# Mixture-of-experts on chip: experts ranked by load, the four emptiest in 64 slots with high and low parts side by side, interleaved chunk by chunk with 128-slot experts

## The reference

```python
def swiglu(h, wg, wu, wd):
    return (jax.nn.silu(h @ wg) * (h @ wu)) @ wd

def moe_swiglu(h, w_router, wg, wu, wd):
    xt = h.reshape(-1, D)                       # 256 x 1024
    logits = (xt @ w_router).astype(jnp.float32)
    top_v, top_i = lax.top_k(logits, TOP_K)     # 2 of 8 experts
    gates = jax.nn.softmax(top_v, axis=-1)
    gate = jnp.sum(jax.nn.one_hot(top_i, N_EXPERTS, ...) * gates[..., None], axis=1)
    for e in range(N_EXPERTS):                  # wg, wu: 1024 x 3584; wd: 3584 x 1024
        y = y + gate[:, e:e + 1] * swiglu(xt, wg[e], wu[e], wd[e])
```

## Time and profile before

| What | Value |
|---|---|
| Median of 3 runs | 1669.54 us (1669.48 to 1670.12) |
| Span of the profiled execution, first to last instruction | 1666.4 us |
| PE busy | 1623.5 us, 97% |
| PEld, DVE, ACT busy | 1347.1, 1317.3, 1082.2 us |
| Mean granted PE clock | 0.988 |
| Read from HBM | 460.18 MB, 277 GB/s over the span |

### The profile page before, as it was taken

The page is one execution under the profiler, slowest core; times in us unless marked ns, Lnnn a source line. Parts: engine busy times, 40 slices in busy tenths (PEclk is TensorE's granted clock), DMA queues, the critical chain, the costliest instruction groups (busy, mean ns, idle before and its releaser), DMA issues.

```text
span 1666.4 us, 20534 instructions
## 1 busy us (share of the span) xinstructions
PE 1623.5 (97%) x7691; PEld 1347.1 (81%) x7691; DVE 1317.3 (79%) x1520; ACT 1082.2 (65%) x1315; POOL 122.1 (7%) x244
## 2 busy tenths in 40 slices
PE   6999999999999996999999999999999999999996
PEld 5788888888888885888888888888888888888884
DVE  4776676575554567898998998998998998998997
ACT  4664574644443562777777777776776776777774
POOL 3433432010000101000000000000000000000000
PEclk9999999999999997999999999999999999999998
DMA  9547445446465633799999999999999999999993
GB/s 347 184 130 216 142 135 177 132 141 202 131 215 189 208 102 102 267 373 381 359 370 337 354 367 371 362 367 333 353 369 373 354 375 338 355 369 355 374 363 131
DMA packets 152928, 462.58 MB, mean 278 GB/s; under 512 B 7870, under 2 KB 12236, under 8 KB 152700
## 3 DMA queue, kind: packets, MB, share of 16 engines
q1 hardware_dynamic: 150384, 454.32, 75.5%
q0 software_dynamic: 1824, 5.11, 1.2%
q10 hardware_dynamic: 620, 1.83, 0.3%
HBM read 460.18 MB, written 1.05 MB: 277 GB/s over the span
## 4 chain that ended last, share of the span: by engine, by line
PE 93%; DVE 3%; DMA 2%; DVEq 1%; issue 1%; ACT 1%; SPq 0%; ACTq 0%
PE ps L2324 19%; PE ps L2322 19%; PE ps L2323 18%; PE ps L1840 8%; PE ps L1842 8%; PE ps L1841 8%; DMA raw_sb<-w_in 2%; PE ps L2349 1%; PE ps L2258 1%; PE ps L1886 1%; PE ps L1888 1%; PE ps L1887 1%; PE ps L1921 0%; DVE wlo_sb L1132 0%; PE ps L1865 0%
## 5 line engine op out<-in xcount | busy, mean ns | idle before, releaser
L1140 DVE TENSOR_TENSOR wlo_sb<-raw_sb,whi_sb 128x1024 fp32r<-128x1024 f32 x672 | 789.0, 1220 | 96.6 <-ACT whi_sb L818 95.5
L818 ACT ACTIVATE whi_sb<-raw_sb 128x1024 fp32r<-128x1024 f32 x672 | 674.9, 1053 | 243.3 <-PE ps L2324 243.3
L2322 PE MATMUL ps<-whi_sb,xlo_sb 128*128 128x512 f32 x896 | 351.2, 392 | 0.9 <-ACT xhi_sb L1076 0.9
L2324 PE MATMUL ps<-whi_sb,xhi_sb 128*128 128x512 f32 x896 | 349.1, 390 | 0.0
L2323 PE MATMUL ps<-wlo_sb,xhi_sb 128*128 128x512 f32 x896 | 348.9, 389 | 0.0
L1132 DVE TENSOR_TENSOR wlo_sb<-raw_sb,whi_sb 128x1024 fp32r<-128x1024 f32 (+2 forms) x198 | 230.1, 1204 | 143.0 <-ACT whi_sb L810 142.0
L810 ACT ACTIVATE whi_sb<-raw_sb 128x1024 fp32r<-128x1024 f32 (+2 forms) x198 | 192.3, 1022 | 160.4 <-PE ps L1842 131.2
L1840 PE MATMUL ps<-whi_sb,xlo_sb 128*128 128x512 f32 (+2 forms) x544 | 213.1, 392 | 4.0 <-DVE xlo_sb L1179 4.0
L1842 PE MATMUL ps<-whi_sb,xhi_sb 128*128 128x512 f32 (+2 forms) x544 | 209.0, 384 | 0.0
L1841 PE MATMUL ps<-wlo_sb,xhi_sb 128*128 128x512 f32 (+2 forms) x544 | 208.7, 384 | 0.0
L2322 PEld LDWEIGHTS ps<-whi_sb,xlo_sb 128*128 128x128 f32 x896 | 168.3, 188 | 35.3 <-issue 1.1
(11 more groups left out here) (351 smaller groups left out, 1514.4 us busy)
## 6 DMA issues: line engine op xcount, KB each, us to landing
raw_sb<-moe_wg SPq DMA_DIRECT2D x115, 1024.0 KB, 5.8
raw_sb<-moe_wu SPq DMA_DIRECT2D x112, 1024.0 KB, 6.0
raw_sb<-moe_wd SPq DMA_DIRECT2D x112, 1024.0 KB, 6.3
raw_sb<-w_in SPq DMA_DIRECT2D x40, 1024.0 KB, 5.2
raw_sb<-w_out SPq DMA_DIRECT2D x16, 1024.0 KB, 5.0
raw_sb<-ffn_wg SPq DMA_DIRECT2D x10, 1024.0 KB, 5.0
raw_sb<-ffn_wu SPq DMA_DIRECT2D x10, 1024.0 KB, 5.2
raw_sb<-ffn_wd SPq DMA_DIRECT2D x10, 1024.0 KB, 5.0
```

The costliest lines, as they stand in the source:

```text
L818: nc.scalar.activation(whi[i % SPLIT][:, c:c + KC // 2, :], raw[i % RAW][:, c:c + KC // 2, :], ACT.Copy).then_inc(hi_ready, 1)
L1140: op = V.tensor_tensor(wlo[i % SPLIT][:, c:c + KC // 2, :], raw[i % RAW][:, c:c + KC // 2, :], whi[i % SPLIT][:, c:c + KC // 2, :], ALU.su ...
L2322: mm(out, lo, whi[q % SPLIT][:, w, :], start=first, stop=False)
L2324: op = mm(out, hi, whi[q % SPLIT][:, w, :], start=False, stop=last)
```

## The change

- DVE ranks the experts by load on the chip (`kinds`): expert 0 is always heavy; of the others, four are light (64 slots, `LIGHT`), and the rest heavy (128 slots). It works out the table `jobs` with the places of all experts (`extras`, `table`). Experts with more tokens than slots would get further pairs. The three parts are done after DVE's splits of steps 0, 1 and 2 of the first pair, which always has expert 0 as its heavy job, and the gates (`gates`) at step 8.
- A light expert has its 64 tokens' high parts and its 64 tokens' low parts side by side in the 128 columns of the stationary side. Two passes, with `whi` and with `wlo`, then give all four products, and the two halves of 64 rows are added by a small matmul with the constant `fold` (which also transposes), for gate and for value. Silu, product and split of a light block work on the transposed 128 x 256 numbers.
- The two jobs of a pair are interleaved chunk by chunk: `FIRST_ORDER` for the first pair (12 heavy chunks first, 12 light last), `PAIR_ORDER` for the others.
- All gate and value chunks are now 512 columns wide, `BLOCKS` = 7 blocks of 4 chunks (rows of 2 KB); the 14 down chunks stay at 4 KB rows.
- SP reads the expert's number from `jobs` and uses it in the address of all loads after the first heavy expert.
- Three memsets on POOL go, the constants of this stage are loaded by POOL just before it, and the other constants in two loads on ACT's queue rather than one.

```diff
-BLOCKS = 4
+BLOCKS = D_FFE // NC
+LEAD = 12
+FIRST_ORDER = [0] * LEAD + [0, 1] * (len(JOB) - LEAD) + [1] * LEAD
+PAIR_ORDER = ([0, 0, 1, 1, 0, 1, 0, 1] + [0, 1] * 4 * (BLOCKS - 2) + [0, 1, 0, 0, 1, 0, 1, 1]
+              + [0, 0, 0] + [1, 0] * (len(JOB_DOWN) - 3) + [1, 1, 1])
...
+            def light_step(i, chunk):
+                out = acc[:, LIGHT_JOB]
+                for c in range(chunk.k):
+                    k = chunk.k0 + c
+                    both = alT[:, k * PART:(k + 1) * PART] if chunk.which == "d" else xhi[:, k, PART:2 * PART]
...
+                        mm(o, both, whi[i % SPLIT][:, w, :], start=first, stop=False)
+                        op = mm(o, both, wlo[i % SPLIT][:, w, :], start=False, stop=last)
...
+            def fold(out, src):
+                for a in range(NC // PART):
+                    op = mm(out[:, a * LIGHT:(a + 1) * LIGHT], src[:, a * PART:(a + 1) * PART], C("fold"), start=True,
+                            stop=True)
...
+            def pair(j):
+                srcs = [expert(expert_at(2 * j + b)) for b in range(2)]
+                for i, step in enumerate(PAIR.steps):
+                    sp_chunk(sp, srcs[step.b][step.chunk.which], AT_MOE, i, step.chunk, PER, j)
...
+                    dve_lo_moe(dve, i + SPLIT, j)
...
+                    if first(j):
+                        if i == 0:
+                            kinds()
+                        if i == 1:
+                            extras()
+                        if i == 2:
+                            table()
...
+                    if i == plan.scat_h + 1:
+                        scattered(2 * j + 1, col_of(2 * j))
```

More of the change, by code:

```diff
@@ L42 @@
 HD = 64
+LIGHT = 64
 COLS = {}
@@ L80 @@
 N_CONST = _at
+N_KEPT = CONST["causal"][0]
+N_MIX = CONST["before"][0]
 def shape_constants():
@@ L201 @@
[L201 to L209, removed]
+HEAVY_JOB, LIGHT_JOB = 0, 1
+ROUNDS = 4
+Step = namedtuple("Step", "b chunk")
+Plan = namedtuple("Plan", "steps gate value fold_g silu_l after_value product_l split_l y_out pick gather back scat_l scat_h")
@@ new lines, with plan_of, ends, both @@
+PAIR_ORDER = ([0, 0, 1, 1, 0, 1, 0, 1] + [0, 1] * 4 * (BLOCKS - 2) + [0, 1, 0, 0, 1, 0, 1, 1]
+              + [0, 0, 0] + [1, 0] * (len(JOB_DOWN) - 3) + [1, 1, 1])
+def plan_of(order, first):
+    steps = merged(order)
+    def ends(b, which, later=0):
+        return {i + later: s.chunk.block for i, s in enumerate(steps)
+                if s.b == b and s.chunk.which == which and s.chunk.last}
+    def both(which, later=0):
+        return tuple(ends(b, which, later) for b in (HEAVY_JOB, LIGHT_JOB))
+    up_end = max(max(ends(b, "u")) for b in (HEAVY_JOB, LIGHT_JOB))
+    y_out = {i: b for b in (HEAVY_JOB, LIGHT_JOB) for i in ends(b, "d")}
+    gather = {up_end + 4 + r: r for r in range(ROUNDS)}
+    scat_h = max(min(y_out) + 2, max(gather) + 2)
+    return Plan(steps, both("g"), both("u"), ends(LIGHT_JOB, "g", 1), ends(LIGHT_JOB, "g", 2), both("u", 1),
+                ends(LIGHT_JOB, "u", 2), ends(LIGHT_JOB, "u", 3), y_out, up_end + 1, gather, LEAD if first else 6,
+                None if first else 1, scat_h)
@@ L589, in rows, with first @@
             return cut
+        def first(j):
+            return isinstance(j, int) and j == 0
         def sp_part(sp, chunks, srcs, c0, per=0, l=0):
@@ L647, in sync_program @@
                 with sp.Fori(EXPERTS // 2, n_pairs) as j:
-                    for b in range(2):
-                        e = sp.value_load(jobs[0:1, bass.ds(2 * j + EXPERT_AT + b, 1)], min_val=0, max_val=EXPERTS - 1)
-                        expert(b, j, e)
+                    pair(j)
             with sp.Else():
@@ L1077, in gathered @@
                                      ACT.Copy).then_inc(xg_hi, 1)
             for r in range(ROUNDS):
[L1080 to L1096, removed]
+                gathered(0, r, (0, PART))
@@ L1117, in scalar_program @@
             with act.Fori(WRITTEN_OUT, n_pairs) as j:
-                for b in range(2):
-                    job(b, j)
+                pair(j, PAIR)
             act.wait_ge(x_final, 1)
@@ new lines, in heavy_waits @@
+            def heavy_waits(chunk, j):
+                done, p = BLOCKS * j, chunk.block
+                if chunk.which == "d":
+                    if chunk.first:
+                        pe.wait_ge(hg_silu, done + BLOCKS)
+                        pe.wait_ge(h_act, done + BLOCKS)
+                    if chunk.k0 * PART % NC == 0:
+                        pe.wait_ge(h_lo, done + chunk.k0 * PART // NC + 1)
+                elif chunk.first and p == 0 and not first(j):
+                    pe.wait_ge(yg_lo, 4 * j)
+                elif chunk.first and p:
+                    pe.wait_ge(hg_silu if chunk.which == "g" else h_act, done + p)
@@ L2350, in job @@
[L2350 to L2364 removed]
+                        elif not first(j):
+                            pe.wait_ge(scat_used, 2 * j + 1)
```

651 lines of the change are left out of this document (403 added, 248 removed).

## The result

| | before | after |
|---|---|---|
| Median | 1669.51 us | 1615.53 us (1614.82 to 1617.06) |
| Ratio, 95% interval | 1 | 0.9681 (0.9667 to 0.9694) |
| Span, mean granted clock | 1666.4 us, 0.988 | 1613.2 us, 0.986 |
| First to last matmul of the experts' stage | 981.4 us | 926.9 us |

What follows compares the result with a forecast made beforehand. The prediction took the kernel as bound by PE before and by the DMA after. Profiled span 1666.4 - 66 + 4 (start) + 2.4 (end) + 4 (handing over) - 8 (head start) = 1602.8, median 3.1 over: 1606 us, range 1580 to 1650.

Steps and rivals of the forecast that it cites:

- So the DMA ends last (229): Experts' stage, per pair: DMA 229 us, DVE 4% under it, PE 7%; gain 16.4 a pair, 66 in four.
- the forecast's signs of a DMA limit: New profile: ACT waiting for raw loads, SP's wait for DVE shrunk, loads landing later than 6 us after issue.
- The DMA's rate: Experts' weight loads: 378 GB/s taken for 2 KB rows, 399 for 4 KB rows, 375 to 395 over the stage.
- the ceiling of 373: Rival: DMA in the stage tops out at 373 GB/s, 236 us a pair, 1634 us in all; chance 0.14.
- the slow rows of 2 KB: Rival: gate and value loads run at 341 GB/s, 247.5 us a pair, 1680 us in all; chance 0.05.
- the rule against the change: Skill's HBM limit of about 358 GB/s per core: 352.3 MB take 984 us, so the change would bring nothing.
- New chains of waits: Rival: in light blocks PE's fold waits for ACT's copy, 1.9 us per light gate, 52 in all, 1658; chance 0.04.
- Folds: PE's 56 light-block folds a pair: 0.13 us each, 7.3 taken, up to 14.6.
- The head start of 8 us: Stage start: nine chunks already landed, 24 us of DMA time, of which 8 are taken off the total.
- The start: Ranking between DVE's splits of chunks 3 to 6: PE stands some 5 us; plus 5, less 1 for a zero scatter.
- The end: After the stage's last matmul, DVE does the heavy job's additions ahead of the result's split: plus 2.4 us.
- PE and DVE set the pace: Rival: queued 2 KB rows also go at 399 GB/s, DMA 221, DVE 219 a pair; 1570 us in all; chance 0.12.

Runs made afterwards that it cites:

- late folds: Against the changed kernel, light folds, silu, product and split come one step later, and ACT's silu stands ahead of its value copy; 1594.79 us, ratio 0.9564.

## Why the prediction came so near, and which step of it failed

The time came within 10 us, and the step that bore it did not hold; that the number did is luck. By its own steps:

- **"So the DMA ends last (229)" failed.** The stage's first matmul is at 664.79, those of pairs 2, 3 and 4 are

```profile
903.14 0.47 PE L2483 MATMUL ps<-whi_sb,xlo_sb 128*128 128x512 f32 x1 [0.22 <-DVE wlo_sb L1268]
...
1131.29 0.39 PE L2483 MATMUL ps<-whi_sb,xlo_sb 128*128 128x512 f32 x1
...
1361.32 0.39 PE L2483 MATMUL ps<-whi_sb,xlo_sb 128*128 128x512 f32 x1
```

  and the last one starts at 1591.67: 238.4, 228.2, 230.0 and 230.4 us. Three of the four are as forecast. But halved loads change nothing, and 20 us go when the copy and the fold are parted. What the stage lasts is PE's own steps (216 a pair by the corrected sum below, 864 of 926.9 us) and its stops, of which the loop with ACT is the largest that a run took away; by chance the two together end where the DMA's price was put. Two of the forecast's signs of a DMA limit came all the same: SP's wait for DVE shrank (790.8 to 697.3), and loads land 7.7 us after their issue at the median, 6.1 before. They show a fuller queue, not a limit.
- **The DMA's rate was right**: 378 and 399 GB/s were taken, full windows of the changed kernel read 382 and 388, and 395 with late folds. So the ceiling of 373 and the slow rows of 2 KB are out, and so is the rule against the change. The Trainium skill (DMA: Bandwidth & Descriptors, Specifications) puts the HBM's limit at about 358 GB/s per core, and its section Bandwidth says that this is each core's part when both cores of a pair read. Here 388 and 395 went over 100 us, with one core at work. (In the rival on rows of 2 KB one figure is off: with 390 for down, as there, 245 a pair is reached under 346 GB/s, not 343.)
- **"New chains of waits" (0.04) was the mechanism**, and its reasoning against itself ("each link has a chunk's time") the error: the chunk's time is there only if ACT is not behind. ACT waits with its split until PE frees a buffer, so it is always close behind PE, and what stands after a split in its order comes a split late. Its price was 1.9 us a light gate, 52 in all; it measured 20. The longest of PE's waits for the gate's copy is 0.8 us (1.2 by the weight loads), not 1.9, because ACT is at the split already when PE has still a chunk to do.
- **Folds were mis-sized**: 7.3 us a pair was taken, 0.92 x 14 = 12.9 measured, within the bound of 14.6. The transposes went the other way, 0.35 for four instead of 0.52: 2.8 instead of 4.2. The forecast's 0.13 is the row's length, 1.03, over eight, and up to the next matmul's start it is 0.79 (693.35 to 694.14). The gathers were read by their length too; from start to start four take 0.48 (687.67 to 688.15), 3.8 a pair instead of 5.1. PE's sum becomes 216 instead of 213. (At the 0.80 of the late folds, fourteen times four folds are 11.2.) DVE's sum was right: 870.5 us busy in the stage is 217.6 a pair, 219.3 forecast.
- **The head start of 8 us was not had.** It was worked out for a DMA that is the limit. The stage was to become 66 - 4 - 4 + 8 = 66 us shorter and became 54.5 (981.4 to 926.9): 11.5 short. All of it lies in the first pair: the terms give it 229, 4 for the start, 1 for handing over and 8 off, so 226, and it took 238.4; the other three, at 230 each, together took 1.5 less than forecast. Of the first pair's 12.4 us 8 are the size of this term. The ranking is another part: without it the first pair takes 232.3 us, 6 less, where 4 was forecast. Its stop for DVE at 896.23 (2.65 us), among the 12 light chunks at its end, is not in the forecast.
- **The start** ("PE stands some 5 us before chunk 6") was right in size and place: 4.5 us; the run without the ranking is 3.9 faster as a whole. The clock fell in that stop, one of the things listed as making the prediction wrong, but cost little: some 8 matmuls 0.2 us late each.
- **The end** (plus 2.4) measured 2.6.
- **Loads by a register's address** at nothing: an issue takes 0.37 us as in the earlier trace rows:

```profile
671.38 0.37 SPq L667 DMA_DIRECT2D raw_sb<-moe_wg  x1
```

- **"PE and DVE set the pace" (1570)** is out for the changed kernel. With late folds PE, DVE and DMA are near their limits at once (98 to 99% and 95 to 97% busy, 386 and 395 GB/s in the two windows), and 1594.8 still is 25 us above that rival's time.

Together: stage +11.5, start of the stage at 664.79 rather than 666.42 -1.6, after the last matmul 21.5 instead of 18.6 + 2.4: +0.5, median over span 2.3 instead of 3.1: -0.8. This makes the 9.6 us over 1606.

## What to carry to other kernels

Where an engine both feeds a ring and does small work that another engine of the ring waits for, its place in the order decides: behind a split that waits for a buffer, a copy of 0.6 us becomes a stop of PE. Leave a step more between the copy and its user, or put the copy first; either gave the same 20 us here. And a DMA share of 1.05 is no proof of a DMA limit: look for the row in which an engine waits for a load, and when several limits lie within a few per cent, take work from each one alone and see what it brings.

## What the runs showed of the hardware

- A float32 matmul with 64 columns from a 128x128 stationary side is recorded as two passes and took 0.23 us from start to start behind a wait and 0.20 without one; a transpose of 128 columns, also from a float32 128x128 stationary side, took 0.09 (0.35 for four).
- After a stop of 4.5 us at the start of the stage, PE's matmuls start 0.43 apart, the lower of its clock's two levels, 1.2 GHz, where 0.227 is the upper, 2.4 GHz; the window from 672 to 690 us reads 0.91. In the run with two passes in the heavy chunks PE was busy 87 and 88% of two steady windows and the granted clock in them read 0.97.
- Loads of 1 MiB ran at 386 GB/s with late folds over 100 us (900 to 1000) in which all 38 loads issued have rows of 2 KB, and at 395 where 20 of 37 have (1200 to 1300), where the same two windows of the changed kernel read 382 and 388: those were what the ring asked for, not what the DMA could give.
